# Stepping a chunked scan and its group norm between units of attention, with the inverses, the branch products and a small projection moved too

## The reference

```python
h = rmsnorm(x) ;  z = h @ w_in            # latents for attention | r, k, v, ranks for RWKV | 2 x 1024 gates
q, k, v = from the latents (8 heads, 96 wide with rotated part; v 64 wide)
y_a = causal_block_attention(q, k, v) @ w_o_mla       # 128 queries at a time over the keys before them
# RWKV-7: state S_t = S_{t-1} diag(decay_t) + (S_{t-1} a_t) b_t^T + v_t k_t^T ;  y_t = S_t r_t
y = group_norm(y per head) * ln_w + ln_b ;  y = (y + bonus) * g
y_b = y @ w_o_rwkv
x = x + (sigmoid(z_a) * y_a + sigmoid(z_b) * y_b) @ w_out
x = x + relu(rmsnorm(x) @ w_ffn_up)^2 @ w_ffn_down
x = x + sigmoid(rmsnorm(x) @ w_ple_gate) * (p @ w_ple_proj)
out = rmsnorm(x)
```

## Time and profile before

| | |
|---|---|
| median of 3 runs | 3375.48 us |
| the profiled execution | 3381.8 us |
| its span, first to last instruction | 3380.0 us |
| instructions | 38401 |
| mean granted TensorE clock | 0.928 of full speed |
| moved by DMA | 252.8 MB |

### The profile page before, as it was taken

The page is one execution under the profiler, slowest core; times in us unless marked ns, Lnnn a source line. Parts: engine busy times, 40 slices in busy tenths (PEclk is TensorE's granted clock), DMA queues, the critical chain, the costliest instruction groups (busy, mean ns, idle before and its releaser), DMA issues.

```text
span 3380.0 us, 38401 instructions
## 1 busy us (share of the span) xinstructions
PE 2943.4 (87%) x16320; PEld 2376.2 (70%) x16320; DVE 1487.5 (44%) x2170; ACT 767.3 (23%) x1063; POOL 476.3 (14%) x304
## 2 busy tenths in 40 slices
PE   5879899999998599898866557888989999999986
PEld 4767788888887478676644345565778888888875
DVE  6973432332333344465542535566333333333334
ACT  4232211111111310244311103334221111111222
POOL 0001110010011110000001212344211111111223
PEclk7989999999999699999987878899989999999998
DMA  4231111111111132344545620100411111111112
GB/s 156 34 99 43 59 42 50 50 50 50 50 50 38 23 127 93 110 137 139 150 140 183 225 98 16 39 1 16 172 38 38 50 50 50 50 50 50 50 50 75
DMA packets 227640, 252.80 MB, mean 75 GB/s; under 512 B 60816, under 2 KB 172304, under 8 KB 226576
## 3 DMA queue, kind: packets, MB, share of 16 engines
q1 hardware_dynamic: 227472, 250.36, 23.1%
HBM read 185.97 MB, written 64.59 MB: 74 GB/s over the span
## 4 chain that ended last, share of the span: by engine, by line
PE 75%; DVE 12%; issue 4%; ACT 3%; DMA 3%; POOL 3%; SPq 1%; POOLq 0%; DVEq 0%; ACTq 0%
PE bank L638 19%; PE bank L639 19%; PE bank L640 19%; PE bank L2681 2%; PE bank L1779 1%; PE bank L1781 1%; PE bank L1780 1%; PE bank L2658 1%; PE bank L2322 1%; POOL sq_sum L182 1%; PE bank L2667 1%; DVE stat L2739 1%; DVE op_lo L192 1%; PE bank L1980 1%; PE bank L1946 1%
## 5 line engine op out<-in xcount | busy, mean ns | idle before, releaser
L638 PE MATMUL bank<-op_hi,w_hi 128*128 128x512 f32 x1952 | 765.2, 392 | 17.4 <-DVE w_lo L182 11.5
L639 PE MATMUL bank<-op_lo,w_hi 128*128 128x512 f32 x1952 | 763.6, 391 | 0.0
L640 PE MATMUL bank<-op_hi,w_lo 128*128 128x512 f32 x1952 | 763.0, 391 | 0.0
L638 PEld LDWEIGHTS bank<-op_hi,w_hi 128*128 128x128 f32 x1952 | 369.0, 189 | 96.4 <-DVE w_lo L182 12.6
L640 PEld LDWEIGHTS bank<-op_hi,w_lo 128*128 128x128 f32 x1952 | 368.9, 189 | 77.5
L639 PEld LDWEIGHTS bank<-op_lo,w_hi 128*128 128x128 f32 x1952 | 369.1, 189 | 76.4
L638 PE MATMUL bank<-f_hi,w_hi 128*128 128x512 f32 x928 | 364.9, 393 | 20.8 <-DVE hT L182 9.1
L640 PE MATMUL bank<-f_hi,w_lo 128*128 128x512 f32 x928 | 363.6, 392 | 0.0
L639 PE MATMUL bank<-f_lo,w_hi 128*128 128x512 f32 x928 | 363.6, 392 | 0.0
L182 DVE TENSOR_TENSOR w_lo<-w_raw,w_hi 128x2048 fp32r<-128x2048 f32 (+2 forms) x116 | 254.9, 2200 | 184.4 <-ACT w_hi L443 180.5
L182 DVE TENSOR_TENSOR hT<-hT,bank 128x512 f32<-128x512 f32 x256 | 170.5, 686 | 357.4 <-PE bank L640 357.4
(11 more groups left out here) (430 smaller groups left out, 3689.8 us busy)
## 6 DMA issues: line engine op xcount, KB each, us to landing
record<-record_scratch SPq DMA_DIRECT2D x16, 1024.0 KB, 5.3
w_raw<-in_w_ffn_up SPq DMA_DIRECT2D x16, 1024.0 KB, 5.2
w_raw<-in_w_ffn_down SPq DMA_DIRECT2D x16, 1024.0 KB, 5.0
w_raw<-in_w_in SPq DMA_DIRECT2D x13, 1024.0 KB, 5.7
w_raw<-in_w_gate SPq DMA_DIRECT2D x11, 1024.0 KB, 5.1
w_raw<-in_w_up SPq DMA_DIRECT2D x11, 1024.0 KB, 5.1
w_raw<-in_w_down SPq DMA_DIRECT2D x10, 1024.0 KB, 5.0
w_raw<-in_w_in SPq DMA_DIRECT2D x17, 512.0 KB, 4.7
```

Of the source, the lines that this page charges most:

```text
L638: t.matmul(ps[:], hi[:, k, wc], x[0][:, k, xc], start=k == 0, stop=False)
L639: t.matmul(ps[:], hi[:, k, wc], x[1][:, (k + turn) % KD, xc], start=False, stop=False)
L640: last = t.matmul(ps[:], lo[:, k, wc], x[0][:, k, xc], start=False, stop=k == kt - 1)
```

## The change

What it does, part by part:

- **wkv**: the norm of `kk` is taken by heads in columns: eight matmuls against two columns of `headones` give a 128 x 16 tile, whose root, maximum and reciprocal are tiny; VectorE spreads it over 1024 columns, eight matmuls against the identity turn it back, and VectorE multiplies from PSUM. `GATE_LEAD` goes from 2 to 4. The first block of `w_uq` and the q latents are loaded in the last `back`.
- **inverses**: half 0 is solved by VectorE and half 1 by GpSimd, a step at a time between the tiles of q and k (`solve`). The copy of the rotated rows goes from VectorE to ScalarE.
- **attention**: query block outermost, so that all heads of a block follow each other; no row of probabilities is divided; the outputs of eight heads gather in one bank with tokens on the partitions, are divided once for each block, and are turned back by four transposes. Scores have 3 banks, transposes 2, outputs 1, the scan 2.
- **scan and group norm**: `alternate` takes a step of attention and a step of the scan by turns, on all engines but SyncE and GpSimd. The scan takes 5 steps for the off-diagonal quarters and 3 for each chunk; after every fourth chunk its quarter of the tokens is normalised, in 6 steps, by the same columns as `kk`.
- **mix2**: both branch products run one after the other from the start of the stage; `mixb_scratch` goes.
- **ple**: the projection is made after each gate block, in the stage itself; VectorE multiplies from its bank, and `proj_scratch` goes.

```diff
+    def solve(e, S, d):
+        r, n = ru[:, d], nu[:, d]
...
+        for s_ in range(HC - 1):
...
+            tt(e, tv, r[:, 0:i_n, s_:s_ + 1].to_broadcast([P, i_n, t_n]),
+               n[:, s_:s_ + 1, s_ + 1:HC].to_broadcast([P, i_n, t_n]), ALU.mult).then_inc(*S.up())
+            e.wait_ge(*S.last())
+            tt(e, r[:, 0:i_n, s_ + 1:HC], r[:, 0:i_n, s_ + 1:HC], tv, ALU.add).then_inc(*S.up("solved"))
+            yield
...
     def qkv_gpsimd(g):
+        after(g, Sg, Sk)
+        chunks = solve(g, Si.G, 1)
         for h, half in k_tiles:
-            g.wait_ge(*Sq.V.of("q sin", h, half))
+            g.wait_ge(*Sq.A.of("rot", h, half))
...
             tt(g, o, o, mem.rot[half][64:96, :], ALU.add).then_inc(*Sq.G.up("q", h, half))
+            next(chunks, None)
...
-    NB, TURN, WEIGH = 4, 3, 4
-    units = [(h, i) for h in range(NH) for i in range(SJ)]
+    TURN, WEIGH = 2, 3
+    units = [(i, h) for i in blocks for h in range(NH)]
...
+    def attention(softmax, turn, weigh, scale, turn_o):
+        for n in range(len(units) + WEIGH + 3):
+            if n < len(units):
+                softmax(n, *units[n])
+            if 0 <= n - TURN < len(units):
+                turn(n - TURN, *units[n - TURN])
+            if 0 <= n - WEIGH < len(units):
+                weigh(n - WEIGH, *units[n - WEIGH])
+            done, left = divmod(n - WEIGH - 1, NH)
+            if left == NH - 1 and 0 <= done < SJ:
+                scale(done, blocks[done])
+            done, left = divmod(n - WEIGH - 2, NH)
+            if left == NH - 1 and 0 <= done < SJ:
+                turn_o(done, blocks[done])
+            yield
...
+    def recurrence(ends, scan, norm):
+        for j in range(NPAIR + 1):
+            ends(j)
+            yield
+        for step in range(3 * NC + GN_STEPS):
+            c, k = divmod(step, 3)
+            if c < NC:
+                scan(c, k)
+            g, j = divmod(step - 12, 12)
+            if g >= 0 and j < GN_STEPS:
+                norm(g, j)
+            yield
...
+    def alternate(x, y):
+        more = True
+        while more:
+            more = False
+            for steps in (x, y):
+                if next(steps, x) is not x:
+                    more = True
+            yield
...
     def mix2_tensor(t):
-        for b in range(2):
-            yield from dense(t, T, wt3, b, f2, 4, halves_of([(i * P, 4 * b + i) for i in range(4)], "mix"), None)
+        for w, (x, name, ready) in enumerate(((o_, "mla", lambda k: Sy.V.of("o lo", k)),
+                                              (yr, "rwkv out", lambda k: Sy.V.of("yr lo", k)))):
+            for b in range(2):
+                yield from dense(t, T, wt_o, 2 * w + b, x, 4, halves_of([(i * P, 4 * b + i) for i in range(4)], name),
+                                 ready if b == 0 else None)
...
     def ple_tensor(t):
         for b in range(4):
             yield from dense(t, Sp.T, wt3, B_PLE + b, op2, KD, halves_of([(0, 2 * b), (P, 2 * b + 1)], "ple"),
                              (lambda k: S2.V.of("lo", k)) if b == 0 else None)
+            landed(t, d_ple_in)
+            for n in range(4 * b, 4 * b + 4):
+                i, half = tiles16[n]
+                ps = tile_of(t, "all", "proj", n)
+                for k in range(2):
+                    last = t.matmul(ps[:], mem.w_proj[:, k, i * P:(i + 1) * P], mem.pT[:, k, hs(half)], start=k == 0,
+                                    stop=k == 1)
+                last.then_inc(*Sp.T.up("proj", n))
...
     def ple_vector(v):
-                v.wait_ge(*Sp.G.of("gated", n))
+                v.wait_ge(*A.of("sigmoid", n))
+                v.wait_ge(*T.of("proj", n))
+                tt(v, t[:], t[:], psum.tile("proj", n)[:], ALU.mult).then_inc(*V.up())
...
-        run(ssm_tensor(t), mix_tensor(t), ffn_tensor(t), z_tensor(t), wkv_tensor(t), inv_tensor(t), scan_tensor(t),
-            rout_tensor(t), qkv_tensor(t), att_tensor(t), mix2_tensor(t), ffn2_tensor(t), ple_tensor(t),
+        run(ssm_tensor(t), mix_tensor(t), ffn_tensor(t), z_tensor(t), wkv_tensor(t), qkv_tensor(t),
+            alternate(att_tensor(t), scan_tensor(t)), mix2_tensor(t), ffn2_tensor(t), ple_tensor(t),
             end_tensor(t))
```

More of the change, by code:

```diff
@@ L500, in build @@
     psum = Psum([nc.alloc_psum_tensor(f"bank{i}", [P, HALF], F32) for i in range(8)],
-                {"all": range(8), "low": range(0, 4), "high": range(4, 8), "scores": range(0, 4), "turns": range(4, 6), "values": range(6, 8)})
+                {"all": range(8), "low": range(0, 4), "high": range(4, 8), "six": range(0, 6), "scores": range(0, 3),
+                 "turns": range(3, 5), "values": range(5, 6), "two": range(6, 8)})
     def dram(name, shape):
@@ L2680, in weigh, with turn_o @@
                     t.wait_ge(*A.of("turn", n, 4))
-                last = t.matmul(ps[rows, 0:P], v_tok[:, k, h * VD:(h + 1) * VD], probT[n % NB][:, k, :],
+                last = t.matmul(ps[:, h * VD:(h + 1) * VD], probT[n % NT][:, k, :], v_tok[:, k, h * VD:(h + 1) * VD],
                                 start=k == 0, stop=k == i)
             last.then_inc(*T.up("value", n))
-        yield from steps(softmax, idle, turn, weigh)
+        def turn_o(b, i):
+            ps = tile_of(t, "turns", "o", i)
+            t.wait_ge(*V.of("o", i))
+            for m in range(4):
+                last = t.transpose(ps[:, m * P:(m + 1) * P], mem.o_tok[b % 2][:, m * P:(m + 1) * P], ident[:])
+            last.then_inc(*T.up("o", i))
+        yield from attention(softmax, turn, weigh, idle, turn_o)
     def att_scalar(s):
@@ new lines, in scan_sync, with scan, norm @@
+    def scan_sync(q):
+        def scan(c, k):
+            if k == 0 and 1 <= c <= NC - 3:
+                q.wait_ge(*Sn.V.of("yu", c - 1))
+                q.wait_ge(*Sn.G.of("decayed", c - 1))
+                load_record(q, c + 2)
+        def norm(g, j):
+            if j:
+                return
+            if g == 0:
+                after(q, Sq)
+            else:
+                q.wait_ge(*So.G.of("y", g - 1))
+            for o, src in ((mem.bonus_n, bonus_dram), (mem.gate_n, g_dram)):
+                q.dma_start(o[:], src.rearrange("(k p) t -> p k t", p=P)[:, :, g * 256:(g + 1) * 256]).then_inc(
+                    *d_gn.up(g, by=16))
+        yield from recurrence(idle, scan, norm)
@@ L2895, in ffn2_sync @@
     def ffn2_sync(q):
-        for i in range(6, B_PLE):
+        for i in range(4, B_PLE):
             wt3.load_at(q, i)
```

1165 lines of the change are left out of this document (567 added, 598 removed).

## The result

The changed kernel ran in 3275.8 us (median of 4 runs, 3270.9 to 3280.9), against 3376.9 for the kernel before beside it: a ratio of 0.970, 95% interval 0.968 to 0.972. It is faster, as forecast, but by 101 us and not by 168, and outside the range. The profiled execution took 3270.9 us, its span 3269.1. It is one of the two shorter of the four, and the execution profiled before was 5 us above its median, so the traces differ by 10 us more than the medians do.

The account below looks back on a forecast made before the run. What could be had was idle PE time between dependent steps. Terms of -15, -67, -92, -27 and +33 sum to -168 us from the profiled 3381.8, giving 3214, or 3207 from the median; the 8-in-10 range was 3145 to 3270.

Parts of the forecast that it names:

- wkv: In wkv, the norm by columns and two more leading gate products save 15 us; bounds 0 and 30.
- Its first half: In wkv, replacing the four 6.55 us reciprocals over 1024 columns by tiny column operations saves 8 us.
- Its second half: At wkv's start, two more leading gate products cover PE's 8.7 us wait for the first ranks, worth 7 us.
- Inverses beside q, k, v: Solve laid beside q, k, v: 171.8 us becomes 105 up to the first off-diagonal product, -67; bounds 85 and 125.
- Rival 3: In q, VectorE's and GpSimd's solver halves take turns, so q takes 65 us, not 45; total 3227; chance 0.09.
- The joint stretch: Attention, scan and group norm together: 402.0 us becomes 310, -92, with PE the longer queue; bounds 270 and 360.
- Rivals 1, 2 and 4: 1: joint stretch 360 (0.18); 2: it packs to 270, or ple's banks are no limit (0.15); 4: slower, 3464 (0.02).
- Branch products: Both branch products run one after the other: 128.6 us becomes 102, -27; bounds 92 and 110.
- ple: In ple, the projection made there costs +33 us, as gate blocks wait for PSUM banks; bounds -10 and +45.

Follow-up runs that it names:

- The run by tiles: The changed kernel with each gate tile of ple's last three blocks followed at once by its projection tile, not four then four: 3243.7 us, ratio 0.960.

## Why the prediction was off, step by step

**wkv failed, by 33 us of 57.** Its first half, that the reciprocals' end is worth 8 us, did not come: the new norm cost 1 us beside a lead of two, within the scatter, and 2 to 6 beside four. PE lost in products (the return took 2.9 to 3.8 us a pair, not 2) and in waits for the spread columns (15.1 us) what it won in waits behind the reciprocal (21.3 to 9.8). Its second half is the step that failed outright: "two more gate products at the start cover the 8.7", worth 7 us. The lead costs 15.2. It covers next to nothing (8.3 us are still waited), since the loads that end that wait are issued behind its stores, and the activations of the ranks behind its steps in ScalarE's program; and the absence of the two products from wkv gives nothing back, since PE idles in their place (41.7 us for 30.9). The step from a forecast 7 to -15.2 is 22 us of the 33, the norm's some 9. I had read PE's idle time there as three waits to be shortened, not as room that the gate products were filling.

**Inverses beside q, k, v: mechanism right, size 11 us off.** 14.5 us to the first rotation (priced 18), 56.0 for q (priced 45), 45.2 from there (priced 18 + 24). The mis-sized term is VectorE's: I priced its step of the solve at 0.65 us, and it took 1.51, for GpSimd's rotation sum held its second operation. (VectorE's terms as written add up to 39 us, not 42: 16 x 2.05 and 6.5. The 45 stood on GpSimd's 42.) Rival 3 had the mechanism, but named the wrong partner (GpSimd's half of the solve) and with it 65 us.

**The joint stretch was right**: 307.5 for 310, PE busy 0.92 of it, seven waits for the scaling, 21.1 us where I priced 16. That the two figures lie so close is luck in part: nine of twelve traces of this code have 317 to 322 us, still within the bounds. Rivals 1, 2 and 4 are out here either way. (The busy times of the earlier trace rows from which this part began add up to 500 us, not 496; nothing hangs on it.)

**Branch products: 11 us off, from a mark.** I ended the stage before at its last remainder of the gated sum (2439.4), 3.9 us ahead of the first sum into x, and the stage after at the same event. But before, `w_out`'s first block had waited for those remainders tile by tile, and was nearly done when the last came. After, the last remainder ends at 2284.3, PE is still in that block, and the first sum into x comes 13.1 us later. From the end of the joint stretch to that remainder (priced 102) it took 103.

**ple was right**, +36 for +33: first tiles read at 3116.0, 3151.5, 3189.1 and 3226.6, 35.5 to 37.5 apart where I had 35.2 and up to 3 of clock; three waits of some 6 us. The wait at the end didn't vanish, it is 12.2 us of 20.6. The run by tiles takes the waits away with the order of the products alone: the banks were the cause, as the step had it.

## What to carry to other kernels

Ask of independent products woven into a dependent chain whether they cover its waits before moving them: if TensorE's idle time in the stretch grows by what is moved out, they did. When work is put ahead to cover a wait, follow the load that ends the wait through its DMA queue: it must not stand behind the stores of that work, nor what is done with the loaded data behind the steps of that work on another engine. Where two products share the banks, let the second follow the first tile by tile and not block by block.

## What the runs showed of the hardware

A VectorE operation on two SBUF operands that begins while a GpSimd sum runs ends when that ends or shortly after it (1.35 us for 0.38), whichever operation of the chain it is; those that read a bank keep their 0.70. If VectorE's operation is the first by 0.1 us, it keeps its time and GpSimd's takes longer (2.27 us for 1.29).

VectorE's scaling of 1024 columns in ple, which has one such operand and which the prediction priced at 2.99 us, shows both cases in the changed kernel:

```profile
3132.36 0.75 DVE L187 TENSOR_SCALAR hT<-hT,vec_cols 128x1024 f32<-128x1024 f32 x1 [1.12 <-ACT sq L456]
3132.50 2.88 POOL L182 TENSOR_TENSOR sq_sum<-sq_sum,sq 128x1024 f32<-128x1024 f32 x1 [44.89 <-ACT sq L456]
...
3160.55 2.93 DVE L187 TENSOR_SCALAR hT<-hT,vec_cols 128x1024 f32<-128x1024 f32 x1 [1.12 <-ACT sq L456]
3160.60 2.34 POOL L182 TENSOR_TENSOR sq_sum<-sq_sum,sq 128x1024 f32<-128x1024 f32 x1 [25.23 <-ACT sq L456]
```

It takes 0.75 us where GpSimd's sum of squares follows 0.14 us behind, and 2.93 or 2.98 where that begins within 0.05 us, as in six of the eight here.

The joint stretch, 3022 recorded instructions of one code, took 307.5 us at a granted clock of 0.86 or 317 to 322 at 0.83 to 0.84 in twelve traces. With a second output bank, which took idle time out of it, the clock was 0.91, and it gave back 11 us beyond the waits removed if set against 307.5.
